# Input projection in units of two kinds, 512 columns a product, with later conditioning columns loaded among its products

## The chip, the cores and the metric

One core of one Trainium2 chip. The time is that of one launch of the whole program in device microseconds, a median over runs. TensorE is PE in the profile (its weight loads PEld), VectorE DVE, ScalarE ACT, GpSimd POOL, SyncE SP.

## The reference, cut to what matters

One layer of a hybrid decoder over 2048 prompt tokens and 8 x 4 sample tokens, D = 1024, all in fp32. The parts that the change touches:

```python
mod = (silu(c) @ w_ada + b_ada)                 # 9 conditioning vectors, w_ada is 1024 x 6144
shift1, scale1, gate1, shift2, scale2, gate2 = six columns of 1024
h = rms_norm(x, norm1_g) * (1 + scale1) + shift1
q, k, v, u, vg = split(h @ w_in)                # w_in is 1024 x 2560, 512 columns each
q, k = rms_norm per head;  vn = rms_norm(gelu(vg)) per group
o_mlp = gelu(u) * (causal(w_s) @ vn + b_s)
```

Behind that stand stick-breaking attention, the output projection and the gated MLP; they use `gate1`, `shift2`, `scale2` and `gate2` and are the same in both kernels.

## The kernel before, in words

The program is a row of blocks; every engine leaves a block before any enters the next.

`prepare` (line 59) loads the nine conditioning vectors, normalises the first pair of token tiles, and computes all 6144 columns of `mod`: eight loads of 128 rows x 6144 columns on SP's queue (lines 99 to 103) into two buffers, twelve matmuls for each (lines 203 to 209), four of which lie side by side in the PE array's 32-column groups. Then rows are copied out, turned by PE, and added to the bias (lines 235 to 248). ACT's queue carries the small loads (lines 158 to 176).

`project_in` (line 382) multiplies the tokens by `w_in`. Tokens are worked in eight pairs of 128-token tiles (p = 0 to 7); a sample group of 32 tokens stands ahead of the last pair. For the kinds u, g, q and k a block scheme with seven products in place of eight is used (`multiply`, line 522): token blocks A11 to A22 (tile by half of the depth), weight blocks B11 to B22 (half of the depth by half of the kind's 512 columns), sums of token blocks S1 to S4 made by POOL ("sums", lines 829 to 841), weight differences T2 to T4 and an altered B12 made once by DVE ("tdiff", lines 761 to 769). Each product is 4 matmuls of 256 columns, named by its number: 1, 2, 6, 5, 7, 3, 4. ACT takes products 1, 6, 5 and 4 out of PSUM, DVE adds 2, 7 and 3. Kind v is two plain products of 8 matmuls of 512 columns.

The order of everything is one list of events (`in_events`, line 280); every engine walks through it and does its own events in that order, with semaphores between. For each pair these are, besides the products: "gelu", "square", "reduce", "hroot", "hnorm", "gain" (the norms of g, q and k: ACT, ACT, DVE, ACT, DVE, POOL), "mix" and "om" (spatial gate: PE, DVE), "turn" and "copy" (transposes on PE, copies on ACT, then a store by SP). For the next pair they are "nsq", "fold", "stat", "root", "invert", "scale", "modulate", "sums": squares on ACT, folded by POOL, summed over partitions by PE in two halves ("stat"), root on ACT, inverse on DVE, scaling on POOL, modulation on ACT (8 operations), sums on POOL. SP walks through the list as well: it stores what is done and loads the x of the pair after the next. The turned `q` and `k` share one buffer (`turned`), so the copy of `k` waits until `q` is stored ("copy", lines 728 to 746).

Attention, which follows, first loads the stored `q` and `k`.

## Time and profile before

| what | value |
|---|---|
| median of 3 runs | 3398.88 us (3394.89 to 3402.58) |
| the profiled execution's own time | 3389.23 us |
| its span, first to last instruction | 3387.4 us |
| PE busy | 3220.9 us (95%) |
| DVE / ACT / POOL busy | 1702.8 (50%) / 1136.5 (34%) / 1576.8 (47%) us |
| mean granted clock of PE | 0.98 |

PE in 40 slices of 85 us: `4899999899999899899999999999999999999999`. The first digit is the preparation; the input projection ends in the eighth slice. A busy PE here counts each matmul's record; in fp32 one matmul leaves two records, so "x16" is eight matmuls. A record reaches some tenths of a microsecond past the start of the next, so rates are read from start to start. "<-" names what the idle time before a row ended with.

### The profile page before, as it was taken

The page shows a single profiled execution, that of the slowest core. Times are in us where ns is not written, and L with a number is a line of the kernel's source. Part 1 is how long each engine was busy: PE and PEld are TensorE (multiplying, and loading weights), DVE is VectorE, ACT ScalarE, POOL GpSimd, SP SyncE. Part 2 cuts the span into 40 slices and gives each one's busy share as a digit, 9 for nine tenths or more (in the row PEclk, how much of TensorE's full clock was granted, in tenths as well). Part 3 has the DMA queues.
Part 4 walks back from the last instruction along what each step waited for, and adds up shares of the span by engine and source line. Part 5 has one row for each costly group of instructions (what it writes and reads, how often), then busy time and mean ns, then how long its engine had stood idle before and what let it go on. Part 6 is the DMA issues. An engine that isn't in the chain of part 4 may idle for free.

```text
span 3387.4 us, 54506 instructions
## 1 busy us (share of the span) xinstructions
PE 3220.9 (95%) x18535; PEld 2426.8 (72%) x18535; DVE 1702.8 (50%) x2588; ACT 1136.5 (34%) x2457; POOL 1576.8 (47%) x1265
## 2 busy tenths in 40 slices
PE   4899999899899899999999999999999999999999
PEld 1688877656556577777777777777777778777777
DVE  0522221288788644535445553543554445666565
ACT  0333433388798623212102321210331220232220
POOL 0322232066566545545435554544554454565553
PEclk7999999999999999999999999999999999999999
DMA  8321111121100167777796767778676765122222
GB/s 339 127 78 44 44 56 64 41 73 51 41 13 14 61 225 263 242 260 257 261 316 207 241 231 238 235 256 292 213 244 228 238 223 163 69 87 75 75 75 81
DMA packets 233252, 536.89 MB, mean 158 GB/s; under 512 B 27407, under 2 KB 57343, under 8 KB 214025
## 3 DMA queue, kind: packets, MB, share of 16 engines
q1 hardware_dynamic: 197206, 354.11, 32.0%
q10 hardware_dynamic: 35763, 179.23, 14.7%
q8 instruction: 151, 2.47, 0.3%
q14 instruction: 132, 1.08, 0.1%
HBM read 498.70 MB, written 34.55 MB: 157 GB/s over the span
## 4 chain that ended last, share of the span: by engine, by line
PE 56%; DVE 6%; issue 2%; ACT 1%; DMA 0%; DVEq 0%; ACTq 0%
PE ff_pB L1602 48%; PE s_pZ L1198 4%; PE s_pO L1212 3%; DVE ff_conv L1894 1%; DVE s_left L1276 1%; DVE ff_act_in L1910 0%; DMA ff_w<-in_w_units 0%; PE s_pZ L1204 0%; ACT ff_conv L1686 0%; DVE ff_conv L1896 0%; DVE ff_x L1821 0%; DVE ff_rs L1903 0%; DVE s_kpage L1887 0%; DVE s_kpage L1884 0%; DVE s_stop L1280 0%
## 5 line engine op out<-in xcount | busy, mean ns | idle before, releaser
L1602 PE MATMUL ff_pB<-ff_act_in,ff_w 128*128 128x256 f32 (+1 forms) x2496 | 613.8, 390 | 21.4 <-ACT ff_act_in L1681 14.6
L1602 PEld LDWEIGHTS ff_pB<-ff_act_in,ff_w 128*128 128x128 f32 x2496 | 473.3, 193 | 131.4 <-issue 45.7
L1950 POOL TENSOR_TENSOR ff_sums<-ff_w 128x512 f32<-128x512 f32 (+1 forms) x152 | 190.9, 1256 | 692.4 <-PE ff_pB L1602 564.4
L1894 DVE SCALAR_TENSOR_TENSOR ff_conv<-ff_raw,k_vecT,ff_conv 128x512 f32<-128x512 f32 x352 | 377.0, 1071 | 91.9 <-ACT ff_raw L1693 85.7
L1821 DVE SCALAR_TENSOR_TENSOR ff_x<-ff_pB,k_mod,ff_x 128x256 f32<-128x256 f32 (+2 forms) x448 | 214.1, 480 | 383.8 <-PE ff_pB L1602 381.0
L1092 POOL TENSOR_TENSOR at_stop<-at_stop,at_left 128x512 f32<-128x512 f32 (+3 forms) x320 | 311.0, 996 | 185.1 <-ACT at_stop L1031 179.1
L1602 PE MATMUL ff_pB<-ff_diff_up,ff_sums 128*128 128x256 f32 (+1 forms) x1600 | 388.0, 384 | 6.3 <-DVE ff_diff_up L1797 6.3
L1716 ACT ACTIVATE ff_raw<-ff_pB 128x256 f32<-128x256 f32 (+1 forms) x352 | 135.6, 387 | 761.2 <-PE ff_pB L1602 755.6
L1602 PEld LDWEIGHTS ff_pB<-ff_diff_up,ff_sums 128*128 128x128 f32 x1600 | 300.8, 190 | 70.6 <-issue 17.9
L1870 DVE TENSOR_TENSOR ff_raw<-ff_raw,ff_pB 128x256 f32<-128x256 f32 (+1 forms) x264 | 111.3, 424 | 474.8 <-PE ff_pB L1602 474.8
L1962 POOL TENSOR_TENSOR ff_raw<-ff_raw,ff_conv 128x512 f32<-128x512 f32 (+1 forms) x88 | 119.1, 1353 | 299.4 <-ACT ff_raw L1699 122.8
L1602 PE MATMUL ff_pB<-ff_hidden,ff_w 128*128 128x256 f32 (+1 forms) x1056 | 257.2, 385 | 0.6 <-DVE ff_x L1821 0.5
L1686 ACT ACTIVATE ff_conv<-ff_raw,k_vecT 128x512 f32<-128x512 f32 (+1 forms) x176 | 144.3, 820 | 283.2 <-DVE ff_raw L1870 280.4
L1080 DVE TENSOR_TENSOR_SCAN at_left<-at_go,at_left,at_one 128x512 f32<-128x512 f32 x192 | 234.7, 1264 | 2.5 <-ACT at_go L1031 1.0
L1602 PEld LDWEIGHTS ff_pB<-ff_hidden,ff_w 128*128 128x128 f32 x1056 | 198.9, 190 | 40.7 <-issue 8.3
L1955 POOL TENSOR_TENSOR ff_sums<-ff_w,ff_sums 128x512 f32<-128x512 f32 (+1 forms) x152 | 220.9, 1453 | 11.9
L1953 POOL TENSOR_TENSOR ff_sums<-ff_w 128x512 f32<-128x512 f32 (+1 forms) x152 | 209.7, 1380 | 11.9
L1602 PE MATMUL ff_pB<-ff_diff_down,ff_sums 128*128 128x256 f32 (+1 forms) x768 | 188.8, 389 | 22.9 <-DVE ff_x L1821 21.3
L1951 POOL TENSOR_TENSOR ff_w<-ff_w 128x512 f32<-128x512 f32 (+1 forms) x152 | 205.1, 1350 | 0.0
L1031 ACT ACTIVATE at_go<-at_pZ,at_bias 128x512 f32<-128x512 f32 (+3 forms) x320 | 185.6, 646 | 47.8 <-PE at_pZ L974 37.2
L1602 PE MATMUL ff_pB<-ff_act_in,ff_sums 128*128 128x256 f32 (+1 forms) x832 | 200.5, 384 | 0.0
L1602 PE MATMUL ff_pB<-ff_diff_up,ff_w 128*128 128x256 f32 (+1 forms) x800 | 193.5, 384 | 0.0
(242 smaller groups left out, 5049.2 us busy)
## 6 DMA issues: line engine op xcount, KB each, us to landing
ff_w<-in_w_units ACTq DMA_DIRECT2D x136, 1024.0 KB, 5.9
s_kpage<-in_cache_k SPq DMA_DIRECT2D x512, 256.0 KB, 4.0
s_vpage<-in_cache_v SPq DMA_DIRECT2D x512, 256.0 KB, 3.1
wada<-in_w_ada SPq DMA_DIRECT2D x8, 3072.0 KB, 12.9
ff_w<-in_w_units ACTq DMA_DIRECT2D x16, 768.0 KB, 4.8
in_w<-in_w_in SPq DMA_DIRECT2D x5, 2048.0 KB, 18.7
in_hT<-in_x_cols SPq DMA_DIRECT2D x8, 1024.0 KB, 6.8
ff_x<-in_x_cols ACTq DMA_DIRECT2D x12, 512.0 KB, 7.4
```

Of the source, the lines that this page charges most:

```text
L1031: ins = act.activation(into[:, s % RS, e, c:KC], pZ[:, s % 2, e, c:KC], ACT.Sigmoid, scale=scale, bias=bias[:, sign, 2 * p + e:2 * p + e + 1])
L1080: dve.tensor_tensor_scan(left[:, e, x0:x1][:, ::-1], go[:, r, e, c:KC][:, ::-1], other, first, ALU.mult, ALU.bypass).then_inc(left_ready, 1)
L1092: pool.tensor_tensor(w, w, left[:, e, x0 + 1:x1 + 1], ALU.mult).then_inc(w_ready, 1)
L1602: last = pe.matmul(into, left[:, kt * P:(kt + 1) * P], right[:, kt, :], start=kt == 0 and p in (1, 2, 5), stop=kt == depth(j) - 1, skip_gr ...
L1686: act.activation(conv[:, f % 2, half, 0:width(c)], raw[:, f % 2, half, 2:2 + width(c)], ACT.Identity, scale=k["vecT"][:, 196 + ft:197 + ft ...
L1716: act.activation(dst, C if p == 5 else A, ACT.Copy).then_inc(taken, 1)
L1821: dve.scalar_tensor_tensor(x[:, d, lo:hi], bank[:, 0:hi - lo], mod, x[:, d, lo:hi], ALU.mult, ALU.add).then_inc(added, 1)
L1894: ins = dve.scalar_tensor_tensor(cv, raw[:, f % 2, half, i:i + CT], tap, cv, ALU.mult, ALU.add)
L1950: pool.tensor_tensor(S3, A11, A21, ALU.subtract).then_inc(sums_ready, 1)
L1951: pool.tensor_tensor(A21, A21, A22, ALU.add).then_inc(sums_ready, 1)
L1953: pool.tensor_tensor(S2, A21, A11, ALU.subtract).then_inc(sums_ready, 1)
L1955: pool.tensor_tensor(S4, A12, S2, ALU.subtract).then_inc(sums_ready, 1)
```

## The change

The first block computes only `shift1` and `scale1` (2048 columns, 8 loaded slices in four loads, a buffer each) and loads the weights of u and g. The other 4096 columns are computed in `project_in`: sixteen 1 MB loads into one buffer on SP's queue, each issued when the product on the slice before is done, and each used by a "mod" event of four matmuls on PE behind products 5 and 3 of both units in pairs 1 to 4. After eight of them DVE copies the rows out ("mrow"), PE turns them ("mturn"), DVE adds the bias ("madd").

The block scheme works on two kinds side by side: u with g, q with k. Its column halves are the two kinds, so a product is 4 matmuls of 512 columns and a pair has 14 such products (28 of 256 before) and the two of v. Products 1, 2, 4 give the first kind, 6, 5, 7, 3 the second. The altered B12 is half the depth of g and of k, and the sample group undoes it with four extra steps. Two sets of weight differences of 4 x 512 columns a partition take the place of four sets of 4 x 256. The event list has a new order. Small constants that are used late, and the eight copies that build the sample gate, go from ACT's queue in the first block to SP's in the second.

The diff, cut (the rest follows from renamed units, new semaphores and wider tiles):

```diff
@@ -96,12 +96,11 @@
             x_cols = a["x_cols"].rearrange("(t p) q -> p t q", p=P)
             sp.dma_start(nxt["hT"][:, 0, :, :], x_cols[:, :, 0:2 * P]).then_inc(nxt["x_loaded"][0], 16)
 
-            for kt in range(KT):
-                if kt >= 2:
-                    sp.wait_ge(mod_part, kt - 1)
-                src = a["w_ada"][0].rearrange("(t p) n -> t p n", p=P)[kt]
-                sp.dma_start(wada[:, kt % 2, :], src).then_inc(wada_loaded[kt % 2], 16)
+            for n in range(4):
+                src = a["w_ada"][0].rearrange("(t p) n -> p t n", p=P)[:, 2 * n:2 * n + 2, 0:2 * D]
+                sp.dma_start(wada[:, 2 * n:2 * n + 2, :], src).then_inc(wada_loaded[n], 16)
             load_in_weights(sp, a, nxt, "u")
+            load_in_weights(sp, a, nxt, "g")
             sp.dma_start(nxt["hs"][:], x_cols[:, :, SEQ:SEQ + S]).then_inc(nxt["xs_loaded"], 16)
             sp.dma_start(nxt["hT"][:, 1, :, :], x_cols[:, :, 2 * P:4 * P]).then_inc(nxt["x_loaded"][1], 16)
...
+            def condition(kt):
+                if kt % 2 == 0:
+                    pe.wait_ge(wada_loaded[kt // 2], 16)
+                for n in range(4):
+                    q = 32 * n
+                    last = pe.matmul(pMod[q:q + 32, :], cT[:, kt, :], wada[:, kt, n * 512:(n + 1) * 512],
+                                     start=kt == 0, stop=kt == KT - 1)
+                return last
+
+            pe.wait_ge(tpose_read, 1)
+            for kt in range(KT - 2):
+                condition(kt)
             pe.wait_ge(vec_loaded, 16 * 7)
...
-            pe.wait_ge(tpose_read, 1)
-
-            for kt in range(KT):
-                pe.wait_ge(wada_loaded[kt % 2], 16 * (kt // 2) + 16)
-                for n in range(12):
-                    q = 32 * (n % 4)
-                    last = pe.matmul(pMod[q:q + 32, n // 4, :], cT[:, kt, :], wada[:, kt % 2, n * 512:(n + 1) * 512],
-                                     start=kt == 0, stop=kt == KT - 1)
-                last.then_inc(mod_part, 1)
+            for kt in range(KT - 2, KT):
+                last = condition(kt)
+            last.then_inc(mod_part, 1)
             pe.wait_ge(tpose_read, 5)
-            for b, bank in enumerate((pT[:, 0, :], pT[:, 1, :], pT2[:])):
-                pe.wait_ge(mod_out, b + 1)
-                for s in range(4):
-                    last = pe.transpose(bank[:, s * P:(s + 1) * P], mod_rows[:, b, s * P:(s + 1) * P], ident[:])
-                last.then_inc(modT_done, 1)
+            pe.wait_ge(mod_out, 1)
+            for s in range(4):
+                last = pe.transpose(pT[:, 0, s * P:(s + 1) * P], mod_rows[:, s * P:(s + 1) * P], ident[:])
+            last.then_inc(modT_done, 1)
...
@@ -273,7 +270,10 @@
 
 
 IN_KINDS = "ugqkv"
+
+IN_PAIRED = {"ug": 3 * DSB, "qk": 0}
...
-        events += [m("u", 1), m("u", 2), *late[0], *once(("tdiff", "g")), m("u", 6), m("u", 5), *late[1], *once(("nsq", SAMPLE, 0)),
-                   m("u", 7), *late[2], m("u", 3)]
-        events += [m("g", 1), m("u", 4), ("gelu", p, "u"), *once(("stat", SAMPLE, 0), ("root", SAMPLE)), m("g", 2),
-                   *once(("tdiff", "q"), ("invert", SAMPLE)), m("g", 6), *ahead(("nsq", 0), ("fold", 0)), m("g", 5),
-                   m("g", 7), m("g", 3), *ahead(("stat", 0))]
-        events += [m("q", 1), m("g", 4), ("gelu", p, "g"), *ahead(("nsq", 1), ("fold", 1)), m("q", 2), *once(("tdiff", "k")), m("q", 6), m("q", 5), *ahead(("stat", 1)),
-                   ("square", p, "g"), ("reduce", p, "g"), m("q", 7), ("hroot", p, "g"), *ahead(("root",)), m("q", 3), ("hnorm", p, "g"),
-                   ("gain", p, "g"), *ahead(("invert",), ("scale",))]
-        events += [m("k", 1), m("q", 4), m("k", 2), m("k", 6), ("square", p, "q"), ("reduce", p, "q"), m("k", 5), ("hroot", p, "q"),
-                   m("k", 7), ("hnorm", p, "q"), ("mix", p), *ahead(("modulate",)), m("k", 3), ("om", p)]
-        events += [m("v", 0), ("turn", p, "om"), ("copy", p, "om"), *ahead(("sums",)), m("k", 4), ("square", p, "k"), ("reduce", p, "k"), ("turn", p, "q"),
-                   ("hroot", p, "k"), ("copy", p, "q"), ("hnorm", p, "k"), ("gain", p, "k"), m("v", 1)]
+        events += [m("ug", 1), m("ug", 2), *late[0], *once(("nsq", SAMPLE, 0)), m("ug", 6), *late[1], *once(("stat", SAMPLE, 0), ("root", SAMPLE)),
+                   m("ug", 5), *once(("invert", SAMPLE)), *ahead(("nsq", 0), ("fold", 0)), m("ug", 7), *late[2], m("ug", 3), *ahead(("stat", 0)),
+                   *once(("tdiff", "qk"))]
+        events += [m("qk", 1), ("gelu", p, "g"), ("square", p, "g"), ("reduce", p, "g"), m("ug", 4), ("gelu", p, "u"), ("hroot", p, "g"),
+                   ("hnorm", p, "g"), ("gain", p, "g"), m("qk", 2), *ahead(("nsq", 1), ("fold", 1)), m("qk", 6), *ahead(("stat", 1), ("root",)),
+                   m("qk", 5), ("mix", p), ("om", p), *ahead(("invert",), ("scale",)), m("qk", 7), m("qk", 3), ("turn", p, "om"), ("copy", p, "om")]
+        events += [m("v", 0), ("square", p, "k"), ("reduce", p, "k"), ("hroot", p, "k"), m("qk", 4), ("hnorm", p, "k"), ("gain", p, "k"),
+                   ("square", p, "q"), ("reduce", p, "q"), *ahead(("modulate",), ("sums",)), ("hroot", p, "q"), m("v", 1), ("hnorm", p, "q"),
+                   ("turn", p, "q"), ("copy", p, "q")]
...
-IN_EVENTS = in_events()
+def with_conditioning(events):
+
+
+    placed, n, since = [], 0, None
+    for event in events:
+        placed.append(event)
+        if event[0] != "mul":
+            continue
+        b = 1 + (n - 1) // KT
+        if since is not None:
+            since += 1
+            if since == 2:
+                placed.append(("mturn", b))
+            if since == 4:
+                placed.append(("madd", b))
+                since = None
+        if event[1] in range(1, 5) and event[2] in IN_PAIRED and event[3] in (5, 3):
+            placed.append(("mod", 1 + n // KT, n % KT))
+            n += 1
+            if n % KT == 0:
+                placed.append(("mrow", n // KT))
+                since = 0
+    return placed
+
+
+IN_EVENTS = with_conditioning(in_events())
...
@@ -439,11 +464,14 @@
         def statistics(p, kind):
             return nth("reduce", p, kind)
 
-        def weights_of(kind):
-            col = IN_COLUMNS[kind]
+        def weights_of(unit):
+            col = IN_PAIRED[unit]
             lo, hi = slice(0, halfk), slice(halfk, KT)
-            left, right = slice(col, col + HC), slice(col + HC, col + DSB)
+            left, right = slice(col, col + DSB), slice(col + DSB, col + 2 * DSB)
             return (w[:, lo, left], w[:, lo, right], w[:, hi, left], w[:, hi, right])
...
-            for kind in "gqkv":
+
+            def load_ada(b, kt):
+                if kt:
+                    sp.wait_ge(mod_done, KT * (b - 1) + kt)
+                elif b > 1:
+                    sp.wait_ge(mod_turned, b - 1)
+                src = a["w_ada"][0].rearrange("(t p) n -> t p n", p=P)[kt][:, 2 * D * b:2 * D * b + 2 * D]
+                sp.dma_start(ada[:], src).then_inc(ada_loaded, 16)
+
+            for kind in "qkv":
                 load_in_weights(sp, a, nxt, kind)
+            load_ada(1, 0)
+
...
+            for b in range(NSEQ):
+                late(k["bs_s"][S + TS * b:S + TS * b + TS, :], a["bs_cols"][0:TS, :])
+            late(k["bias"][:, 0, :], a["sb_bias"][0:1, :].to_broadcast([P, H]))
+            for r in range(0, P, 32):
+                for t in range(TS):
+                    late(k["bias_s"][r + t:r + 32:TS, 0:1], a["sb_bias"][0].rearrange("(h a) -> h a", a=1))
+            late(k["pt"][:], a["page_table"].rearrange("(a b) n -> a (b n)", a=1))
+            for b in range(NSEQ):
+                sp.dma_start(k["wd"][TS * b:TS * b + TS, :, TS * b:TS * b + TS], k["wsT"][0:TS, :, 0:TS]).then_inc(nxt["wd_loaded"], 16)
...
+                if name == "mod" and which[1] + 1 < KT:
+                    load_ada(which[0], which[1] + 1)
+                if name == "mturn" and which[0] == 1:
+                    load_ada(2, 0)
...
-                        into = slice(HC, DSB) if n >= KT else slice(0, HC)
+                    many = "guqv" if unit == "ug" else "k"
+
+                    own = {one: [(one, kt) for kt in range(KT)] for one in many}
+                    for one, other in (("g", "u"), ("k", "q")):
+                        if one in many:
+                            own[one] += [(other, kt) for kt in range(halfk)]
+                    for n in range(KT + halfk):
                         for one in many:
-                            if one == "v" and n >= KT and half == 0:
-                                continue
-                            col = IN_COLUMNS[one] + HC * half
-                            last = pe.matmul(bank[rows_at(p, one), into], hs[:, kt, :], w[:, kt, col:col + HC], start=first, stop=final)
+                            if n < len(own[one]):
+                                of, kt = own[one][n]
...
+                S1, S2, S3, S4 = (ss[:, n, :, :] for n in range(4))
                 if p == 0 and part in (6, 7, 4):
-                    pe.wait_ge(diffs_ready, 4 * (IN_KINDS.index(kind)) + {6: 3, 7: 3, 4: 4}[part])
-                T2, T3, T4 = (tw[kind][:, n, :, :] for n in range(3))
+                    pe.wait_ge(diffs_ready, diffs_before(unit) + {6: 3, 7: 3, 4: 4}[part])
+                T2, T3, T4 = (tw[unit][:, n, :, :] for n in range(3))
                 left, right = {1: (A11, B11), 2: (A12, B21), 6: (S2, T2), 5: (S1, B12), 7: (S3, T3), 3: (S4, B22), 4: (A22, T4)}[part]
                 for kt in range(halfk):
-                    last = pe.matmul(bank[:, 0:HC], left[:, kt, :], right[:, kt, :], start=kt == 0 and part in (1, 2, 5), stop=kt == halfk - 1,
+                    last = pe.matmul(bank[:], left[:, kt, :], right[:, kt, :], start=kt == 0 and part in (1, 2, 5), stop=kt == halfk - 1,
                                      skip_group_check=part in (6, 7, 4, 3))
...
+                elif name == "mod":
+                    b, kt = which
+                    pe.wait_ge(ada_loaded, 16 * IN_AT[event])
+                    if kt == 0 and b > 1:
+                        pe.wait_ge(mod_added, b - 1)
+                    for n in range(4):
+                        last = pe.matmul(pM[32 * n:32 * n + 32, :], cT[:, kt, :], ada[:, 512 * n:512 * n + 512], start=kt == 0, stop=kt == KT - 1)
+                    last.then_inc(mod_done, 1)
+                elif name == "mturn":
+                    pe.wait_ge(mod_rows, which[0])
+                    for n in range(4):
+                        last = pe.transpose(pM[:, n * P:n * P + P], ada[:, n * P:n * P + P], k["ident"][:])
+                    last.then_inc(mod_turned, 1)
                 elif name == "stat":
                     p, half = which
                     if roots_before(p):
...
+            act.activation(k["bias"][:, 1, :], k["bias"][:, 0, :], ACT.Copy, scale=-1.0)
+            act.activation(k["bias_s"][:, 1:2], k["bias_s"][:, 0:1], ACT.Copy, scale=-1.0)
 
```

## Rows read from the trace of the kernel before

**Rows 1.** Timeline of PE up to pair 1: start, us, operation, tiles, [idle before <-releaser]

```profile
65.43 2.78 PE L207 MATMUL prep_pMod<-wada,cT 128*32 128x512 f32 x24 [2.13 <-DMA wada<-in_w_ada]
...
93.69 5.38 PE L563 MATMUL in_pB<-in_w,in_hT 128*128 128x256 f32 x16 [3.26 <-ACT in_hT L703]
...
101.49 3.45 PE L563 MATMUL in_pB<-in_t_u,in_sums 128*128 128x256 f32 x8 [2.42 <-issue]
...
135.78 0.67 PE L589 MATMUL in_pS<-in_sq,k_ones 128*128 128x256 f32 x2 [2.33 <-POOL in_sq L822]
...
170.83 3.62 PE L563 MATMUL in_pB<-in_w,in_hT 128*128 128x256 f32 x16
```

**Rows 2.** Windows, start: us, busy time of PE, PEld, DVE, ACT, POOL; clock, DMA, GB/s

```profile
0.00:10.00 10.00, 1.86 (x10) 1.71 (x11) 1.72 (x3) 3.40 (x3) 2.29 (x14) 1.00 0.77 269
...
10.00:20.00 10.00, 4.69 (x15) 3.15 (x14) 1.75 (x1) 2.81 (x3) 1.78 (x1) 0.96 1.03 431
...
100.00:110.00 10.00, 8.51 (x33) 7.31 (x34) 6.19 (x5) 1.07 (x3) 1.31 (x2) 0.83 1.04 387
```

**Rows 3.** Timeline of SP's DMA issues and of ACT around the projection's start

```profile
79.25 5.70 SPq L106 DMA_DIRECT2D in_hT<-in_x_cols  x1
...
91.47 4.04 ACT L703 ACTIVATE in_hT<-in_hT,k_mod,k_gain 128x256 f32<-128x256 f32 x8 [43.03 <-PEq L64]
```

**Rows 4.** Timeline of DVE and POOL in pairs 0 and 2

```profile
132.89 2.17 DVE L769 TENSOR_TENSOR in_t_k<-in_w 128x1024 f32<-128x1024 f32 x1
...
268.17 1.27 POOL L820 TENSOR_TENSOR in_sq<-in_sq 128x512 f32<-128x512 f32 x1 [8.17 <-ACT in_sq L690]
...
269.51 0.72 POOL L822 TENSOR_TENSOR in_sq<-in_sq 128x256 f32<-128x256 f32 x1
...
275.23 1.23 DVE L801 TENSOR_TENSOR in_raw_g<-in_raw_g,in_hrstd 128x1024 f32<-128x1024 f32 x1
...
276.53 2.35 POOL L852 TENSOR_TENSOR in_raw_g<-in_raw_g,k_vg 128x1024 f32<-128x1024 f32 x1 [6.29 <-DVE in_raw_g L801]
```

**Rows 5.** Timeline of PE in pair 2, and ACT's copy of that product

```profile
286.60 1.89 PE L563 MATMUL in_pB<-in_w,in_sums 128*128 128x256 f32 x8
...
288.33 7.03 PE L554 MATMUL in_pB<-in_w,in_hT 128*128 128x512 f32 x16
...
295.46 0.60 ACT L660 ACTIVATE in_raw_v<-in_pB 128x512 f32<-128x512 f32 x1 [7.04 <-PE in_pB L554]
```

**Rows 6.** Timeline of ACT in pair 2

```profile
266.09 1.06 ACT L707 ACTIVATE in_raw_g<-in_raw_g 128x1024 f32<-128x1024 f32 x1
...
272.33 1.28 ACT L726 ACT_TABLE_LOAD   x1
```

**Rows 7.** Timeline of PE after two waits, windows after the first and at 136

```profile
1817.78 5.38 PE L1602 MATMUL ff_pB<-ff_act_in,ff_w 128*128 128x256 f32 x16 [3.28 <-ACT ff_act_in L1681]
...
2929.10 10.07 PE L1602 MATMUL ff_pB<-ff_act_in,ff_w 128*128 128x272 f32 x32 [3.42 <-ACT ff_act_in L1681]
...
1818.00:1821.00 3.00, 3.00 (x8) 2.39 (x8) 2.97 (x5) 2.41 (x6) 1.85 (x3) 0.50 0.01 3
...
136.00:139.00 3.00, 3.00 (x15) 2.64 (x15) 2.08 (x3) 2.42 (x3) 0.00 (x0) 1.00 0.00 0
```

**Rows 8.** Timeline of PE and SP, sample group to the end; a DMA issue

```profile
575.07 8.83 PE L543 MATMUL in_pB<-in_w,in_hs 128*32 128x256 f32 x152
...
593.60 3.72 PE L563 MATMUL in_pB<-in_w,in_hT 128*128 128x256 f32 x16
...
601.45 1.91 PE L598 MATMUL in_pX<-in_raw_g,k_wd 32*32 32x128 f32 x8 [4.13 <-POOL in_raw_g L852]
...
668.20 1.04 PE L615 MATMUL in_pX<-k_ident,in_raw_k 128*128 128x128 f32 x8
...
670.06 0.37 SPq L495 DMA_DIRECT2D scratch_kT<-in_turned  x1
...
scratch_qT<-in_turned SPq DMA_DIRECT2D x8, 512.0 KB, 2.9
```

More of the change, by code:

```diff
@@ L518, in _, with multiply @@
             sp.wait_ge(stored["gv"], 16)
+            sp.wait_ge(nxt["late_loaded"], 16 * LATE)
         @block.tensor
         def _(pe):
-            def multiply(p, kind, part):
-                product = (p, kind, part)
-                R, bank = size(p), pB[in_bank(*product)]
-                B11, B12, B21, B22 = weights_of(kind)
+            def multiply(p, unit, part):
+                product = (p, unit, part)
+                bank = pB[in_bank(*product)]
                 if IN_EARLIER[product]:
@@ L543, in multiply @@
-                            last = pe.matmul(bank[rows_at(p, one), into], hs[:, kt, :], w[:, kt, col:col + HC], start=first, stop=final)
+                            if n < len(own[one]):
+                                of, kt = own[one][n]
+                                last = pe.matmul(bank[rows_at(p, one), :], hs[:, kt, :], w[:, kt, IN_COLUMNS[of]:IN_COLUMNS[of] + DSB],
+                                                 start=n == 0, stop=n == len(own[one]) - 1)
                     last.then_inc(prod_done, 1)
@@ L545, in multiply @@
                     return
-                A11, A12, A21, A22 = tokens_of(p)
-                S1, S2, S3, S4 = (ss[:, n, :, :] for n in range(4))
-                if kind == "u" and part in (1, 2):
+                if unit == "ug" and part in (1, 2):
                     pe.wait_ge(h_ready, KT * p + (halfk if part == 1 else KT))
-                if kind == "u" and part == 6:
+                if unit == "ug" and part == 6:
                     pe.wait_ge(sums_ready, 4 * p + 4)
-                if kind == "v":
+                if unit == "v":
@@ L640, in free_raw, with take @@
                         act.wait_ge(turn_done, TURN_AT[earlier, "om", last])
-            def take(p, kind, part):
-                product = (p, kind, part)
-                if part == (0 if kind == "v" else 1):
-                    free_raw(p, kind)
-                bank, into = pB[in_bank(*product)], raw[kind]
-                act.wait_ge(prod_done, prod(product))
+            def take(p, unit, part):
+                product = (p, unit, part)
+                bank = pB[in_bank(*product)]
                 if part == "s":
-                    for one in "vguq" if kind == "g" else "k":
+                    act.wait_ge(prod_done, prod(product))
+                    for one in "vguq" if unit == "ug" else "k":
                         free_raw(p, one)
@@ L654, in take @@
                     return
-                elif kind == "v":
-                    dst, src = into[:, part, :], bank[:]
-                else:
-                    t, half = {1: (0, 0), 6: (0, 1), 5: (1, 1), 4: (1, 0)}[part]
-                    dst, src = into[:, t, HC * half:HC * half + HC], bank[:, 0:HC]
-                act.activation(dst, src, ACT.Copy).then_inc(taken, 1)
+                kind, t = ("v", part) if unit == "v" else {1: (unit[0], 0), 6: (unit[1], 0), 5: (unit[1], 1), 4: (unit[0], 1)}[part]
+                if part in (0, 1, 6) and t == 0:
+                    free_raw(p, kind)
+                act.wait_ge(prod_done, prod(product))
+                act.activation(raw[kind][:, t, :], bank[:], ACT.Copy).then_inc(taken, 1)
             def whole(p, kind):
@@ L668, in complete @@
                 if p == SAMPLE:
-                    drained(act, (p, "k" if kind == "k" else "g", "s"))
+                    drained(act, (p, "qk" if kind == "k" else "ug", "s"))
                 else:
-                    for part in (7, 3, 4):
-                        drained(act, (p, kind, part))
+                    unit = "ug" if kind in "ug" else "qk"
+                    for part in (2, 4) if kind == unit[0] else (7, 3):
+                        drained(act, (p, unit, part))
             for event in IN_EVENTS:
```

143 lines of the change are left out of this document (77 added, 66 removed).

## The prediction

> **What bounds the kernel now.** I read the page's parts first, then PE's timeline stage by stage. Up to 93.69 us PE mostly waits: each round of twelve conditioning products stands behind its DMA, and the projection's first product comes only then [rows 1]. From there PE is the bound: from 170.83 on, six pairs of token tiles follow each other in 404.24 us, 67.37 a pair, to the sample group at 575.07 [rows 1, 8], and the timeline has no idle time of PE between. So the change can win before the first product, and every wait that it puts into a pair is lost time. What comes behind the projection is untouched. Sums are made against the profiled execution, 3389.23 us (span 3387.4); the median of the runs, 3398.88, lies 9.65 above it, and I put the difference on the median. About 0.2%, 6.8 us, is what a measurement can tell from no change.
>
> **Start.** 8.39 MB of conditioning columns come ahead of the projection instead of 25.2. DMA moves 431 GB/s when full, 269 over the first 10 us, 387 with the projection weights' short rows [rows 2]. x, the columns and the small vectors are 10.1 MB, of which 2.7 land in the first 10 us: 10 + 7.4/0.431 = 27.2 us. The `u` weights (2.1 MB) follow at 32.6, `g` at 38.0; with 1.5 for the slowest DMA engine (chosen; bounds 0 and 4) `g` is there at 39.5. The first block ends when SP too has issued its loads, and an issue into a full queue lasts until the queue has drained enough (5.70 us [rows 3]). SP now issues `g`, the sample's x and the next pair's x behind a full queue, so it leaves at about 36.2, when most of `g` has gone through (bounds 34 and 38). Modulation starts at 36.5 instead of 91.47 and lasts 4.04 [rows 3]; products 1 and 2 start 2.2 behind its start, as at 93.69, and run from 38.7 to 47.5: 6.87 and the 1.9 that the slow clock cost the old ones (5.38 us instead of 3.46 [rows 1]).
>
> Product 6 then needs three of the weight differences and all four sums of tokens. A difference now has 2048 elements a partition: twice a DVE operation of 1024 (1.23 [rows 4]) less one overhead, some 2.2. Four of these on DVE and four sums on POOL (1.27 each, as the fold of that shape [rows 4]) fall together, and such operations take turns: a subtraction on DVE beside a fold on POOL lasted 2.17 [rows 4]. In turn they need 4 x 2.2 + 4 x 1.15 = 13.4 us, which puts product 6 at 52.9. Were they free of each other, PE's own end at 47.5 would decide; with `g` late it is 56. I take 52.9, as the row shows the turn-taking for these very operations. The old product 6 started at 101.49 [rows 1].
>
> From there to pair 1 the old kernel takes 69.3 us (to 170.83). The new one has 3.45 less to multiply (its products 1 and 2 were double) and 0.3 less issue, loses the old wait of 2.33 [rows 1], and gains the three losses of the next part, 3.5 + 1.6 + 1.7. In this pair DVE's second set of differences (9 us) also stands ahead of the statistics of `g`, but ends in time not to lengthen the wait by more than some tenths. 52.9 + 70.0: pair 1 at 122.9, **47.9 us earlier**. The late small loads and the gate's small copies go from ACT's queue to SP's, behind the weight loads; the sample group is the first to wait for them, some 500 us on, so they cost nothing, and even late they would hold up only SP's stores.
>
> **Each pair.** A product of four matmuls of 256 columns starts 1.73 after the one before; eight of 512 take 7.03 less the tail of 0.16 (1.89 - 1.73), so a new product lasts 3.43, and the fourteen save 0.3 us in all [rows 5].
>
> The new order puts POOL's gain of `g` ahead of the second fold of the next x, and PE's second statistic, which needs that fold, behind product 6 of `qk`. Count from the start of `qk`'s product 1. It ends at 3.43, and ACT sees it 0.26 later (295.46 against 288.33 + 6.87). ACT takes it (0.60), loads a table (1.28), does gelu and square of `g` (1.06 each), takes product 4 of `ug` (0.60), does gelu of `u` (1.06), loads a table (1.28) [rows 5, 6]; then come root and inverse with all hand-overs (1.0, chosen), DVE's multiplication (1.23), POOL's gain (2.35) and fold (1.27 + 0.72) [rows 4]. That makes 17.2. PE reaches the statistic at 4 x 3.43 = 13.7: a **wait of 3.5 us** in each of the seven pairs that prepare a next one. All that PE has to do stands queued behind it.
>
> After such waits the granted clock was at the lower of its two levels (0.50, 1.2 GHz) for a while: after 3.28 us idle sixteen matmuls took 5.38 instead of 3.62, after 3.42 thirty-two of 272 columns took 10.07 instead of 7.5; after 2.33 it stayed at 1.00 [rows 1, 7]. I take 1.6 a wait (bounds 0 and 2.6), nearest to the row of 3.28.
>
> The turn of `q` now stands behind the second `v` product. From the end of the first: product 4 and its take (3.43 + 0.26 + 0.60), square (1.06), eight modulations (4.04), root, inverse and hand-overs (0.8), and DVE's multiplication (1.23), which takes turns with the sums on POOL for 0.6 more. About 12.0, against 3.43 + 6.87 = 10.3 for PE: a **wait of 1.7** (1.0 without turn-taking). So a pair costs -0.3 + 3.5 + 1.6 + 1.7 = +6.5, six pairs **+39.0**.
>
> **Moved conditioning products.** Pairs 1 to 4 get 16 groups of four matmuls that use 32 columns of the array each. Twelve took 2.78 with the tail [rows 1], so four side by side cost 0.87. With 0.2 for the two edges (chosen between nothing and two tails of 0.16) it is 1.07, and two sets of turns add 0.4 each: **+17.9**. Bounds: 14 with free edges, 55 if the four ran one after the other. The Trainium skill (TensorEngine Tiling, Key Properties) says that changing the tiling mode drains the array; it gives no price. By that rule each edge would take a full tail, 16 x 0.32 = 5.1 us instead of the 3.2 in my sum. No row here shows a lone group between full-array products. Each next 1 MB is issued when SP has seen the group before it done. Half as much lands 2.9 us after its issue [rows 8], so I estimate 4.3; the next group is at least two products, 6.9, away, which hides it. Behind that wait SP has only stores and the next x, and PE waits for none of them soon.
>
> **Sample group, last pair, end.** The sample's two products become twelve steps of 512 columns (10.3) instead of 8.76 each: **+3.1**. In the last pair the sample's mix still comes 7.85 after the pair's start (601.45 - 593.60 [rows 8]). Products 1 and 2 now fill 6.9 of that, so the wait of 4.13 and the slow clock behind it (an estimate of 2.5, from the mix's 1.91 and a product as at 101.49) shrink to waits of 1.0 and 1.3, the second for ACT, and half a chance of 2.4 of clock. With 0.3 of issue and the turn of `q` moved out (0.87): **-4.5**. At the end, the store of kT was issued 1.86 after the last product (670.06 - 668.20 [rows 8]). Both transposed results use one buffer, and `q` now comes last but one: its turn, two copies, its store landed (2.9 [rows 8]), then the copies of `k`: 0.87 + 0.25 + 1.35 + 0.4 + 2.9 + 0.6 = 6.4: **+4.5**.
>
> **Sum:** -47.9 + 39.0 + 17.9 + 3.1 - 4.5 + 4.5 = +12.1 us, which gives 3411.0.
>
> **Rivals.** *The clock holds* through waits of 3.5 us, so the change is not slower. For it: 2.33 us went by without a fall. Against: 3.28 and 3.42 did not. It decides at the first statistic wait; 7 x 1.6 = 11 less, 3400.
> *The turn-taking does not strike*: DVE's big differences and POOL's sums overlap, product 6 at 47.5 (-5.4, and 1.6 of clock), and the turn of `q` is 0.6 earlier seven times: 11 less, 3400. Against it stand the rows above.
> *No statistic wait*, the faster side: the chain from `qk`'s first product to the fold takes under 13.7 us. That would need the gelu of `u` with its take (1.7) and the gain (2.35) off the chain. It saves 7 x 5.1 = 36: 3375. The order in the event list, by which each engine's program is written, speaks against it.
> *The groups of four run in series* when they stand between full-array products: 16 x 2.57 = 41 more, 3452. The old block shows them side by side, but never among such products.
>
> **How the numbers follow.** Forecast 0.50 (own range 3400 to 3424: start 4, clock and edges 8 either way); clock holds 0.20; no turn-taking 0.12; no statistic wait 0.10; series 0.08. The range 3392 to 3430 leaves out the last two. It reaches down to the two small rivals, partly together, and up to a clock loss of 2.6 a wait (+7), `g` late (+3), edges and hand-overs dearer (+9). Faster by over 0.2%: 0.13 (the no-wait case and a corner where small rivals meet). Within 0.2%: 0.33 (most of the small rivals, the forecast's low end). Slower: 0.54.
>
> **What would show it.** The projection's first product at about 38.7, product 6 near 53, pair 1 near 123; seven waits of PE on POOL's fold of some 3.5 us and seven on DVE's multiplication of `q` of some 1.7; a granted clock of 0.50 behind the first kind; 16 groups at about 1.07; the store of kT issued 6.4 after the last product of `v`. If pairs without moved groups last 67 us, or pair 1 starts before 115, the forecast is wrong.

## The result and the profile after

The changed kernel takes 3400.14 us (median of 20 runs, 3396.32 to 3412.06) against 3394.41 for the kernel before on the same chips: a ratio of 1.0019, 95% interval 1.0012 to 1.0026, some 6 us slower. The forecast was 12 slower than before. One execution told of below (the shift by 4) was disturbed as a whole, its matmuls taking twice their usual time, so only the places of its stops are read, never its times, and one of the five of the last run (3925.46 us at a mean granted clock of 0.80) is left out of its ratio.

| | before | after |
|---|---|---|
| profiled execution, span | 3389.23, 3387.4 us | 3397.34, 3395.6 us |
| projection's first product | 93.69 | 39.25 |
| pair 1 starts | 170.83 | 124.62 |
| sample group starts | 575.07 | 585.98 |
| last pair starts | 593.60 | 607.84 |
| attention's first scores | 677.42 | 689.73 |
| feed-forward's first long wait ends | 1250.91 | 1257.09 |

The columns differ by -54.4, -46.2, +10.9, +14.2, **+12.3**, and then **+6.2** us. So the projection and all ahead of it lost what was forecast; half of that came back behind it, where the change touches no line. (The two profiled executions differ by 8.1 us, the medians by 5.7.)

PE's timeline of the changed kernel up to pair 1, for [rows 1] (start, us, operation, tiles, idle before and its releaser):

```profile
39.25 8.62 PE L619 MATMUL in_pB<-in_w,in_hT 128*128 128x512 f32 x16 [5.24 <-ACT in_hT L772]
53.86 6.41 PE L619 MATMUL in_pB<-in_t_ug,in_sums 128*128 128x512 f32 x8 [5.99 <-POOL in_sums L929]
...
79.49 3.60 PE L619 MATMUL in_pB<-in_w,in_hT 128*128 128x512 f32 x8
82.92 3.60 PE L619 MATMUL in_pB<-in_t_qk,in_sums 128*128 128x512 f32 x8
89.88 0.99 PE L658 MATMUL in_pS<-in_sq,k_ones 128*128 128x256 f32 x2 [3.36 <-POOL in_sq L910]
90.67 5.01 PE L619 MATMUL in_pB<-in_w,in_sums 128*128 128x512 f32 x8
...
123.69 1.09 PE L686 MATMUL in_pX<-k_ident,in_raw_q 128*128 128x128 f32 x8 [1.32 <-DVE in_raw_q L885]
```

The new waits stand where they were expected: for the sums ahead of product 6, for POOL's fold ahead of the second statistic, for DVE's norm ahead of the turn of `q`. The product behind the statistic lasts 5.01 instead of 3.60. A window on the next pair's product shows why, with the granted clock (seventh value, behind the five busy times) at 0.50, the 1.2 GHz level:

```profile
166.00:168.00 2.00, 1.93 (x4) 1.26 (x5) 0.00 (x0) 0.47 (x1) 0.00 (x0) 0.50 0.00 0
```

PE's waits from the start to 700 us, as the view of waits groups them (us in all, times, longest):

```profile
PE in_pS L658 <- POOL in_sq L910: 22.9, 7, 3.4
...
PE in_pX L686 <- DVE in_raw_q L885: 8.3, 7, 1.3
...
PE in_pB L619 <- POOL in_sums L929: 6.0, 1, 6.0
PE in_pB L619 <- ACT in_hT L772: 5.2, 1, 5.2
```

DVE's differences and POOL's sums in the first pair, for the row of 2.17 us in [rows 4]:

```profile
40.53 2.29 DVE L853 TENSOR_TENSOR in_t_ug<-in_w 128x2048 f32<-128x2048 f32 x1 [5.90 <-DMA in_w<-in_w_in]
41.16 2.79 POOL L924 TENSOR_TENSOR in_sums<-in_hT 128x512 f32<-128x512 f32 x1 [12.64 <-ACT in_hT L772]
42.86 3.24 DVE L853 TENSOR_TENSOR in_w<-in_w 128x2048 f32<-128x2048 f32 x1
43.91 3.31 POOL L925 TENSOR_TENSOR in_sums<-in_hT 128x512 f32<-128x512 f32 x1
```

They alternate: each ends when the other's has ended and one more operation's time has passed (2.29 alone, 3.24 beside the other engine).

Now the place at which the time came back. Attention is a loop of two turns on every engine, and its code is the same in both kernels. PE's timeline where the loop goes back to its head, **before**:

```profile
917.81 1.97 PE L1002 MATMUL at_pO<-at_wT,at_v 128*64 128x128 f32 x32
922.74 1.13 PE L974 MATMUL at_pZ<-at_kT,at_q 64*128 64x512 f32 x2 [2.96 <-issue]
927.91 1.86 PE L974 MATMUL at_pZ<-at_kT,at_q 64*128 64x512 f32 x2 [4.04 <-issue]
...
934.05 2.08 PE L974 MATMUL at_pZ<-at_kT,at_q 64*128 64x512 f32 x4 [1.94 <-ACT at_stop L1031]
```

and **after**:

```profile
929.89 1.97 PE L1091 MATMUL at_pO<-at_wT,at_v 128*64 128x128 f32 x32
934.57 1.13 PE L1063 MATMUL at_pZ<-at_kT,at_q 64*128 64x512 f32 x4 [2.71 <-issue]
...
939.87 1.98 PE L1063 MATMUL at_pZ<-at_kT,at_q 64*128 64x512 f32 x4 [2.89 <-ACT at_stop L1120]
```

"Issue" is a wait for nothing that the profile shows. The four matmul records of the loop's first product are two float32 matmuls. The old kernel stops twice, 2.96 and 4.04 us, with the first of the two (two records) between; the new one stops once. Behind the second stop the old kernel's granted clock stayed at the lower level until about 941 us; these windows are of before, then of after, at the same distance from the loop's return (the clock is the seventh value again):

```profile
929.00:935.00 6.00, 4.06 (x9) 1.14 (x10) 2.58 (x3) 4.71 (x7) 0.83 (x1) 0.50 0.91 291
935.00:941.00 6.00, 5.77 (x22) 2.66 (x19) 5.87 (x6) 6.00 (x12) 5.59 (x6) 0.52 0.00 1
```

```profile
941.00:947.00 6.00, 4.89 (x24) 2.19 (x22) 5.87 (x6) 6.00 (x11) 5.43 (x6) 0.80 0.93 298
947.00:953.00 6.00, 5.62 (x54) 3.66 (x54) 5.17 (x8) 4.26 (x11) 3.62 (x5) 1.00 0.00 1
```

From the first scores to the end of the feed-forward part's first long wait (4.59 us on ACT) it is 573.5 us before and 567.4 after. This "attention stage" is what the shifts below compare (a shift is a run with instructions added ahead of the loop, so that the loop's head, the first instruction of its body, stands later in PE's program).

The list of DMA queues has one for instructions. Of the old kernel from 925 to 928 us, the time of the second stop, it shows one packet of about 16 KB (packets, MB, share):

```profile
q8 instruction: 1, 0.02, 2.2%
```

### The profile page after: what moved, and what is told of

It reads as the page before. It is cut to its first block, busy times and chain, and to the rows that moved or that the text cites. A ratio compares the mean times of both kernels' runs of the same rounds, so it can differ in the third digit from the quotient of the medians.

```text
span 3395.6 us, 52375 instructions
## 1 busy us (share of the span) xinstructions
PE 3227.9 (95%) x17542; PEld 2251.0 (66%) x17543; DVE 1701.9 (50%) x2532; ACT 1125.2 (33%) x2391; POOL 1589.5 (47%) x1265
## 4 chain that ended last, share of the span: by engine, by line
PE 56%; DVE 6%; issue 1%; ACT 1%; DMA 0%; DVEq 0%; ACTq 0%
PE ff_pB L1691 48%; PE s_pZ L1287 4%; PE s_pO L1301 3%; DVE ff_conv L1983 1%; DVE s_left L1365 1%; DVE ff_act_in L1999 0%; PE s_pZ L1293 0%; ACT ff_conv L1775 0%; DVE ff_conv L1985 0%; DVE ff_x L1910 0%; DVE ff_rs L1992 0%; DVE s_kpage L1976 0%; DVE s_kpage L1973 0%; DVE s_stop L1369 0%; ACT ff_act_in L1770 0%
```

## The experiments

Two questions: are the waits in a pair separate losses, each with its own cure; and is the 6 us behind the projection chance, or the place of PE's instructions?

**The fold earlier.** In the event list the second square and fold of the next x, and its statistic, go ahead of gelu and square of `g`:

```diff
-                   *once(("tdiff", "qk"))]
-        events += [m("qk", 1), ("gelu", p, "g"), ("square", p, "g"), ("reduce", p, "g"), m("ug", 4), ("gelu", p, "u"), ("hroot", p, "g"),
-                   ("hnorm", p, "g"), ("gain", p, "g"), m("qk", 2), *ahead(("nsq", 1), ("fold", 1)), m("qk", 6), *ahead(("stat", 1), ("root",)),
+                   *once(("tdiff", "qk")), *ahead(("nsq", 1), ("fold", 1))]
+        events += [m("qk", 1), *ahead(("stat", 1)), ("gelu", p, "g"), ("square", p, "g"), ("reduce", p, "g"), m("ug", 4), ("gelu", p, "u"), ("hroot", p, "g"),
+                   ("hnorm", p, "g"), ("gain", p, "g"), m("qk", 2), m("qk", 6), *ahead(("root",)),
```

> The kernel after the change, with the second square, fold and statistic of the next pair's x moved ahead of gelu and square of g: the fold no longer stands behind POOL's gain of g. Theory (the wait behind POOL's fold and the slow clock behind it are what a pair lost): the seven waits of 3.25 us shrink under 0.5 each, and the lower clock that followed six of them (1.4 to 2.4 us each) goes with them: 7 x 3.25 = 23 and 6 x 1.8 = 11, some 30 us less than the changed kernel, about 0.993 of the kernel before. Rival (the chain through gelu, root and gain is the real bound; the wait only moves to the gate product behind the gain or to the next pair's sums): under 10 us less, 1.000 or above. The attention stage, from the first product of scores to the first long wait of the feed-forward part, should stay at 567 us as after the change, if instruction placement sets it.

3368.96 us, ratio 0.9926 (0.9914 to 0.9938), 31.2 less than the changed kernel. The first pair still waits, since there the folds take turns with the second set of weight differences (2.45 and 2.65 us instead of 1.26 and 0.72); in all others the statistic follows its product without a gap, and the next product lasts 3.60. The wait row, and pair 1's statistic:

```profile
PE in_pS L658 <- POOL in_sq L910: 3.1, 1, 3.1
```

```profile
152.27 0.67 PE L658 MATMUL in_pS<-in_sq,k_ones 128*128 128x256 f32 x2
152.78 3.60 PE L619 MATMUL in_pB<-in_t_ug,in_hT 128*128 128x512 f32 x8
```

The place in the event list alone made the wait; the rival, that the chain would bind elsewhere, falls.

**The clock alone.** Three matmuls of 512 columns, whose result nobody reads, fill most of that wait on PE, in the bank that the gate product overwrites next:

```diff
                     else:
+                        if half == 1:
+                            turn_waits((p - 1, "mix", 0))
+                            for kt in range(3):
+                                pe.matmul(pX[turn_bank((p - 1, "mix", 0))][:], k["ones"][:], w[:, kt, IN_COLUMNS["q"]:IN_COLUMNS["q"] + DSB],
+                                          start=True, stop=True)
                         pe.wait_ge(folded, 2 * nth("fold", p, half))
```

> The kernel after the change, with three products of 512 columns, whose result nobody reads, on TensorE ahead of each pair's second statistic, so that it works through 2.6 of the 3.3 us in which it waited. The wait's end is set by POOL's fold and stays where it was. Theory (idle time lets the clock fall, and the lower clock costs 1.4 to 2.4 us after six of seven waits): the clock behind the statistic stays at its upper level, 10 us less than the changed kernel, ratio 0.999. Rival (the clock falls for another reason, or that loss is hidden): no difference, 1.002.

3385.25 us, ratio 0.9968 (0.9955 to 0.9981). The attention's first scores come at 679.96 instead of 689.73: 9.8 us earlier. It is clock, since the statistic still starts when the fold ends (41.4 us behind pair 2's start in both kernels). Up to the sample group the gain was 11.5; the last pair gave 1.6 back, as there the clock fell behind a wait of 1.03 (granted 0.57 from 606 to 610 us), which it had not in the changed kernel. (The profiled spans differ by 9.5, the medians by 14.9.) Pair 1's rows, and the last pair's product 6:

```profile
161.26 2.74 PE L660 MATMUL in_pX<-in_w,k_ones 128*128 128x512 f32 x6
164.59 0.70 PE L663 MATMUL in_pS<-in_sq,k_ones 128*128 128x256 f32 x2 [0.59 <-POOL in_sq L915]
165.13 3.60 PE L619 MATMUL in_pB<-in_w,in_sums 128*128 128x512 f32 x8
...
606.38 5.27 PE L619 MATMUL in_pB<-in_t_ug,in_sums 128*128 128x512 f32 x8 [1.03 <-ACT in_raw_u L733]
```

Work that computes nothing made the kernel faster: behind the seven statistics 0.6 to 0.7 us of waiting left no lower clock, 3.25 did in six of seven cases (in five of seven in the next run, whose waits for the fold are the same).

**The root of `q` earlier.**

```diff
-                   ("square", p, "q"), ("reduce", p, "q"), *ahead(("modulate",), ("sums",)), ("hroot", p, "q"), m("v", 1), ("hnorm", p, "q"),
+                   ("square", p, "q"), ("reduce", p, "q"), ("hroot", p, "q"), *ahead(("modulate",), ("sums",)), m("v", 1), ("hnorm", p, "q"),
```

> The kernel after the change, with the square root for q's norm moved on ACT ahead of the next pair's eight modulations. Theory (PE's turn of q waits because that root stands behind the modulations): the seven waits of 0.9 to 1.3 us go, 8 us less, ratio 0.9995 to the kernel before. Rival (the modulations come later by the root and what it waits for, so the sums on POOL and the next pair's product 6 are late instead): no difference or slower, 1.002 or above.

3391.29 us, ratio 0.9989 (0.9978 to 1.0000), 8.9 less than the changed kernel; the wait's row (8.3 us in all) is gone. Of the other waits only those ahead of pair 1 changed by more than some tenths, among them ACT's modulation from 5.2 to 6.8 us and POOL's sums from 6.0 to 3.8. In the profiled execution the scores come 12.9 us earlier: 4.2 of it is product 6 of the first pair, which starts 1.4 earlier and runs at the upper clock (3.67 us instead of 6.41).

**The loop's head in the old kernel.** Instructions that only wait for a semaphore long at its value, ahead of the loop on PE (two waits make one instruction):

```diff
             pe.sem_inc(wT_done, 2 * RS)
+            for _ in range(50):
+                pe.wait_ge(wT_done, 2 * RS)
             with pe.Fori(0, TURNS) as it:
```

> The kernel before the change, with 25 instructions that only wait for a semaphore long at its value put into TensorE's program ahead of the attention loop, in a stretch in which TensorE waits 8.2 us for its keys anyway. Theory (where the loop's head falls among the blocks in which instructions are loaded sets whether TensorE stops once or twice when it goes back to the loop's head; 25 instructions put the head where it is in the changed kernel): the second stop of 4.0 us and the 17 us of lower clock behind it go, the stage from the first product of scores to the feed-forward part's first long wait lasts 567 us instead of 573.5, ratio 0.998. Rival (chance of the run, or an effect of the change's data or order): the stage stays at 573, or anywhere between from run to run, ratio 1.000.

3389.80 us, ratio 0.9987 (0.9978 to 0.9996): the old kernel becomes faster by 4.4 us for 25 instructions more. There is one stop, and the stage lasts 567.8. (This gain is of the medians and of the stage; the profiled execution, 3393.78, took 8.8 us more behind the stage than the old kernel's; why stays open.)

```profile
924.13 1.13 PE L974 MATMUL at_pZ<-at_kT,at_q 64*128 64x512 f32 x4 [2.81 <-issue]
...
929.43 2.00 PE L974 MATMUL at_pZ<-at_kT,at_q 64*128 64x512 f32 x4 [2.89 <-ACT at_stop L1033]
```

To bar chance, the old kernel once more, and shifts by 4, 256 and 512 in the same way.

> The kernel before the change once more, unchanged. Theory (placement): the second stop of TensorE at the attention loop's return is there again, about 4 us, two matmuls behind the first, and the attention stage lasts 573 us. Rival (chance of the run): the stop is missing or elsewhere, the stage nearer 567.

> The kernel before, with 4 instructions ahead of the attention loop on TensorE. Theory (blocks): the second stop comes four instructions, two matmuls, earlier: ahead of or around the loop's first product, and the stage still lasts about 573. Rival (chance): the stage is anywhere from 566 to 574 without a shift of the stop's place.

> The kernel before, with 256 instructions ahead of the attention loop on TensorE. If the blocks that are loaded hold 256 instructions and only the place within one decides, the second stop of 4 us is there, two matmuls behind the first, and the stage lasts 573. The run with 231 instructions in the changed kernel, in which it was absent, speaks for more than that: then it is absent here, stage 566 to 570. The time itself is longer by up to 40 us, by the added instructions.

> The kernel before, with 512 instructions ahead of the attention loop on TensorE. If the second stop needs the same place modulo 512, it is here and not with 256; if modulo 256, in both; if it was chance or depends on the whole place of the program, in neither. The time itself is longer by up to 80 us, by the added instructions.

The old kernel again, the shift by 4, and the shifts by 256 and by 512, each where the loop goes back:

```profile
921.76 1.12 PE L974 MATMUL at_pZ<-at_kT,at_q 64*128 64x512 f32 x2 [2.66 <-issue]
928.03 1.86 PE L974 MATMUL at_pZ<-at_kT,at_q 64*128 64x512 f32 x2 [5.15 <-issue]
```

```profile
1730.22 2.10 PE L974 MATMUL at_pZ<-at_kT,at_q 64*128 64x512 f32 x4 [8.28 <-issue]
```

```profile
946.00 1.12 PE L974 MATMUL at_pZ<-at_kT,at_q 64*128 64x512 f32 x2 [2.92 <-issue]
951.17 1.86 PE L974 MATMUL at_pZ<-at_kT,at_q 64*128 64x512 f32 x2 [4.05 <-issue]
```

```profile
973.40 1.12 PE L974 MATMUL at_pZ<-at_kT,at_q 64*128 64x512 f32 x2 [2.66 <-issue]
979.40 1.86 PE L974 MATMUL at_pZ<-at_kT,at_q 64*128 64x512 f32 x2 [4.88 <-issue]
```

Apart from the shift by 4, the second stop is there each time, 4.05 to 5.15 us, two matmul records behind the first, unchanged by 256 and 512 instructions. These two records are one float32 matmul; with its two weight loads (the pages count as many of these as matmul records) it is four instructions, and four more ahead of the loop moved the stop by just those: both stops fall together, 8.28 us ahead of the loop's first matmul. So the place counts modulo 256. The packets on the queue for instructions, counted over the whole execution, agree: of the old kernel, of its shifts by 256 and by 512, and of a run below in which the changed kernel's head stands at the same place, with 1792 = 7 x 256 instructions fewer ahead of it than in the old one:

```profile
q8 instruction: 151, 2.47, 0.3%
q8 instruction: 152, 2.49, 0.3%
q8 instruction: 153, 2.51, 0.3%
q8 instruction: 144, 2.36, 0.3%
```

One packet of 16 KB is one block of 256 instructions. (Only kernels with the head at one place compare so; the shifts by 25 and by 4 have 152 and 153 as well.) In the old kernel the block that holds the loop's head ends behind the loop's first float32 matmul: PE waits for that block, uses its last few instructions, and waits for the next. The stage lasted 575.7 (again), 572.8 (by 256) and 572.6 us (by 512).

**The loop's head in the changed kernel.** If so, the stop can be given to the new kernel. Places are counted from the first instruction of PE's program and given modulo 256. 131 of the added instructions stand behind the preparation's last turn, 100 ahead of the loop, written as above.

> The kernel after the change, with 231 such instructions (131 behind the preparation's last turn, 100 ahead of the attention loop, both where TensorE waits), which put the loop's head at the same place modulo 256 instructions as in the kernel before. Theory (placement): the second stop comes back, the attention stage lasts 573 us instead of 567, and the whole is 6 us longer than the changed kernel, ratio 1.0037, a little more if the instructions are not hidden. Rival (chance): the stage stays at 567 and the ratio at 1.0019.

3409.73 us, ratio 1.0045 (1.0032 to 1.0058), but with one stop and a stage of 566.3: the added time is that of the added instructions, which were not all hidden (scores at 711.04 in the profiled execution, at 3417.45 the slowest of the five). The expectation missed, and it told against the theory until the count was mended: a float32 matmul is four instructions here, not two, and 231 put the head at 174 modulo 256, not at the old kernel's 142. For the same reason the shift by 25 had put the old head at 167 and not, as expected, at the changed kernel's 199; both are away from 142. At 146, in the shift by 4, the stops fell together ahead of the first matmul; two instructions of address arithmetic stand ahead of it, so that a block ends at place 148.

> The kernel after the change, with 198 such waiting instructions and one signal on TensorE ahead of the attention loop, spread over three stretches in which it waits. Each float32 matmul of the program is two passes with a weight load each, four instructions; counted so, the loop's head stands at 142 modulo 256 in the kernel before and at 199 in the changed one, and 231 were the wrong number (174). With 199 it stands at 142. Theory (place modulo 256): the second stop of 4 to 5 us comes, two matmuls behind the first, and the attention stage lasts 573 to 576 us instead of 567. Rival (something else of the old kernel made the second stop): one stop only, stage 566 to 570.

```diff
+            pe.sem_inc(own, 1)
+            for _ in range(2 * 64):
+                pe.wait_ge(own, 1)
             pe.wait_ge(consts_made, 4)
...
             last.then_inc(modT_done, 1)
+            for _ in range(2 * 44):
+                pe.wait_ge(mod_out, 1)
...
             pe.sem_inc(wT_done, 2 * RS)
+            for _ in range(2 * 90):
+                pe.wait_ge(wT_done, 2 * RS)
```

3411.87 us, ratio 1.0055 (1.0036 to 1.0073): 11.7 over the changed kernel, of which 7.1 stand ahead of the scores (696.78). The second stop is there, in the same place, and the stage lasts 573.3:

```profile
941.01 2.07 PE L1069 MATMUL at_pZ<-at_kT,at_q 64*128 64x512 f32 x2 [2.95 <-issue]
946.46 2.07 PE L1069 MATMUL at_pZ<-at_kT,at_q 64*128 64x512 f32 x2 [3.38 <-issue]
```

That settles it: given to one kernel and taken from the other, the second stop makes stages of 572.6 to 575.7 with it and 566.3 to 570.2 without, over all the profiled executions here but that of the shift by 4. The added instructions do not blur it: counted from the first product behind the first stop, it is 328.2 to 330.5 us in the five executions with the second stop and 322.4 to 324.9 in the seven without.

**All of it together.** The two reorderings, with the first pair's statistic two products later, and the last pair's turned `k` in the free buffer of the other result:

```diff
...
+        stat = ahead(("stat", 1))
+        events += [m("qk", 1), *(stat if p else []), ("gelu", p, "g"), *([] if p else [m("ug", 4), *stat]), ("square", p, "g"), ("reduce", p, "g"),
+                   *([m("ug", 4)] if p else []), ("gelu", p, "u"), ("hroot", p, "g"),
...
-                    dst = omT if use == "om" else turned
+                    dst = omT if use == "om" or (use == "k" and p == NPAIR - 1) else turned
...
-                        act.wait_ge(stored["q"], stores(p))
+                        act.wait_ge(stored["om" if p == NPAIR - 1 else "q"], stores(p))
```

> Fold and root moved ahead together, in the first pair the statistic two products later than in the others (there the fold takes turns with the weight differences and PE waited 3.1 us for it), and at the end the turned k goes to the other result's buffer, so that it doesn't wait for the store of q. Theory (the waits are separate losses): 3369 - 8.9 (turn of q) - 3.1 and some 2.5 of lower clock (first pair) - 2.5 (end) = 3352, ratio 0.988. Rival (one wait hides another): 3360 or above, 0.990.

3355.01 us (3352.93 without the execution left out), ratio 0.9881 (0.9862 to 0.9899): 1.2% faster than the kernel before, 45 us under the changed one. The gains add up as if each wait stood alone. Pairs 5 and 6 start at 404.64 and 471.90 and the sample group at 539.26: 67.3 us a pair, the old kernel's 67.37. The waits ahead of the first pair's product 6 remain:

```profile
PE in_pB L621 <- ACT in_hT L774: 5.0, 1, 5.0
PE in_pB L621 <- POOL in_sums L931: 4.4, 1, 4.4
```

## Why the prediction was right and wrong

**Start.** Right. SP left its issues at 36.62 (31.32 + 5.30; forecast 36.2), the first product came at 39.25 (38.7), product 6 at 53.86 (52.9), pair 1 at 124.62 (122.9): 46.2 us won instead of 47.9. Turn-taking struck as [rows 4] said.

**Each pair.** Right in sum: six pairs grew from 404.24 to 461.36 us, by 57.1, and the forecast had 39.0 + 17.9 = 56.9. Its terms traded a little. A row's idle time starts at the end of the last record, whose tail of 0.16 the forecast counted with the wait. The statistic's wait was 3.25 to 3.36 (3.41 to 3.52 with the tail; 3.5 forecast). The clock: from the statistic's start to the end of the next product took 1.7 us more than in the run with filled waits in five cases, 2.9 in one and nothing in the seventh, 1.60 on the mean (1.6). The turn of `q` waited 0.9 to 1.3, 1.2 on the mean (1.35 with the tail; 1.7). The turn-taking in it was right, for DVE's multiplication of `q` lasted 1.9 beside POOL's sums in all seven pairs, that of `k` 1.2:

```profile
195.41 1.22 DVE L885 TENSOR_TENSOR in_raw_k<-in_raw_k,in_hrstd 128x1024 f32<-128x1024 f32 x1
...
201.51 1.90 DVE L885 TENSOR_TENSOR in_raw_q<-in_raw_q,in_hrstd 128x1024 f32<-128x1024 f32 x1
```

Too dear were root, inverse and hand-overs: 0.5 from the last modulation's end (201.00) instead of 0.8. And in the two pairs with a wait of 0.9 PE turned conditioning rows ahead of the second `v` product.

**Moved groups.** Right but for 1 us. Pairs 2 to 4 last 78.53, pair 5 without groups 73.80: 1.18 a group with its share of the turns (17.9 / 16 = 1.12). One group:

```profile
173.05 1.07 PE L641 MATMUL in_pM<-in_ada,in_cT 128*32 128x512 f32 x8
174.05 2.05 PE L669 MATMUL in_pX<-in_raw_g,k_wsT 128*128 128x128 f32 x16
```

From its start to the next is 1.00. For four side by side [rows 1] give 0.87, so both edges together cost about 0.13. The Trainium skill (TensorEngine Tiling (Array Packing), Key Properties) has a change of the tiling mode drain the array. Two full tails, 0.32, would have been more than the trace shows.

**Sample group, last pair, end.** The first was +3.3 (3.1). From the last pair's start to its last `v` product it is 5.8 less (4.5 forecast; the terms named there add up to 4.3), since its waits were 0.83 and 1.03 and the clock did not fall behind them. The store of kT was issued 6.33 behind that product (6.4). The scores followed that product 13.0 us later instead of 9.2: +3.8 (4.5).

So up to the scores the sum was +12.3, against 12.1 forecast. **The step that failed** is one sentence: "What comes behind the projection is untouched." It put the time behind the projection at no change; the attention stage came out 6.1 us shorter (573.5 to 567.4). Its lines are untouched, but not the place of its instructions. The change takes 1991 instructions from PE's program ahead of the attention loop (6286 to 4295), which moved the loop's head from 142 to 199 modulo 256, away from a block's end (148), and with that went a stop of 4 us with the slow clock behind it. The rows were read up to the projection's end [rows 8]; the wait of 4.04 us with no releaser stood in the timeline of before, in a loop that was thought of no concern. Another 2.0 us of the span were lost behind the stage; that is no more than two executions of the old kernel differ there (2136.5 and 2133.7 us from the first long wait's end to the span's). The medians differ by 2.4 less than the profiled executions, which single executions from 3396 to 3412 us allow.

Of the rivals, "the clock holds" (3400) gave the time that was measured. That is luck: the clock fell in six of seven waits, and its 3400 stood on a median of 3398.88 from three runs, where twenty gave 3394.41.

## What to carry to other kernels

An engine's program has a length as well as an order: where a loop's body is long (here 5476 instructions on PE), look at where its head falls in the blocks of 256 instructions; some waiting instructions ahead of it can be worth several us, and a change elsewhere can give or take them unseen. When operations are moved side by side, write down for each wait which other engine's queue stands ahead of it: here two places in a list were worth 40 us, nearly as much as the start had won (46). Between pieces of work on PE a wait of 3.3 us was dearer by half than it looks (1.6 on the mean), because of the clock behind it.

## What was not expected of the hardware

PE's stop at a loop's return shows no releaser. It was 2.7 to 3.3 us for the first block and another 3.4 to 5.2 for a second that is needed at once, and a packet on the instruction queue lies in the second. The Trainium skill (Runtime: NRT & Kernel Launch, Instruction fetch mechanics) tells of blocks of 16 KB, 256 instructions. The Trainium skill (Runtime: NRT & Kernel Launch, Instruction fetch mechanics) also has a taken branch, where its target is not in the blocks at hand, wait until the target's block is fetched. The shifts by 4, 25, 256 and 512 and the counts of packets agree with both. A wait-only instruction on PE cost about 0.11 us where nothing hid it: from the shift by 256 to that by 512 the first scores moved from 701.89 to 729.87.
